# A decoder trunk step: shift, scale and h in two halves of the channels, with sample states on row groups and moved transposes

## What is computed

```
mod = silu(c) @ w_ada + b_ada
sh1, sc1, g1, sh2, sc2, g2 = split(mod, 6)
h = rmsnorm(x, norm_pre1) * (1 + sc1) + sh1
bg, cg, ua, q, k, v, r, lr, ga, gb = split(h @ w_in, ...)
y_a = bg * causal_dwconv(cg * ua)
log_a = log_sigmoid(lr @ w_a2 + b_a) / 16
S_t = diag(exp(log_a_t)) S_{t-1} + k_t^T v_t;  o_t = q_t S_t      # 4 heads, 128 x 256 states
y_b = rmsnorm(o) * silu(r)
x = x + g1 * rmsnorm((sigmoid(ga) * y_a + sigmoid(gb) * y_b) @ w_out, norm_post1)
h2 = rmsnorm(x, norm_pre2) * (1 + sc2) + sh2
a, gt = split(h2 @ w_up, 2)
x = x + g2 * rmsnorm((gelu(causal_dwconv(a)) * gt) @ w_down, norm_post2)
```

## Time and profile before

| | us |
|---|---|
| median of 3 runs | 1036.38 (1033.21 to 1036.59) |
| the profiled execution | 1031.13 |
| its span, first to last instruction | 1029.4 |
| PE busy | 1004.1 |
| DVE, ACT, POOL busy | 458.1, 368.2, 352.2 |
| mean granted clock of TensorE | 0.993 |

### The profile page before, as it was taken

One profiled execution on the slowest core, in us unless ns is written; L12 is line 12 of the kernel. 1 busy time (PEld: TensorE's weight loads), 2 busy tenths in 40 slices (PEclk: granted clock), 3 DMA queues, 4 the chain that ended last, 5 costly groups with the idle time before them and its releaser, 6 DMA issues.

```text
span 1029.4 us, 19196 instructions
## 1 busy us (share of the span) xinstructions
PE 1004.1 (98%) x7823; PEld 909.4 (88%) x7823; DVE 458.1 (45%) x664; ACT 368.2 (36%) x556; POOL 352.2 (34%) x174
## 2 busy tenths in 40 slices
PE   7799999999999999999999989999999999999997
PEld 5499889999999999989988779999999999888886
DVE  2410204575666554534556767545544445300204
ACT  4433532233434342544443434333333333212212
POOL 2033433242433333233342034333344333333330
PEclk9999999999999999999999989999999999999999
DMA  9658333756664566545354023322222222222212
GB/s 347 173 81 200 106 87 85 142 96 143 176 161 119 134 159 96 135 105 120 103 160 143 1 79 93 95 82 82 82 82 82 82 82 89 74 82 82 84 69 92
DMA packets 143858, 115.33 MB, mean 112 GB/s; under 512 B 11098, under 2 KB 123506, under 8 KB 142770
## 3 DMA queue, kind: packets, MB, share of 16 engines
q1 hardware_dynamic: 143697, 114.38, 42.1%
q10 hardware_dynamic: 96, 0.04, 0.0%
HBM read 107.02 MB, written 7.35 MB: 111 GB/s over the span
## 4 chain that ended last, share of the span: by engine, by line
PE 92%; SPq 3%; DVE 3%; ACT 1%; issue 1%; DMA 0%; DVEq 0%; ACTq 0%
PE pair L1546 60%; PE pair L1598 16%; PE pair L1873 4%; SPq L586 2%; PE pair L1678 1%; PE pair L1651 1%; PE pair L1533 1%; PE pair L1773 1%; SPq L624 1%; PE pair L1590 1%; PE pair L1741 1%; PE pair L1730 1%; PE pair L1591 1%; PE pair L1592 1%; PE pair L1589 1%; SPq L626 1%
## 5 line engine op out<-in xcount | busy, mean ns | idle before, releaser
L761 POOL TENSOR_TENSOR w_lo<-raw,w_hi 128x1024 fp32r<-128x1024 f32 x108 | 263.5, 2441 | 493.9 <-ACT w_hi L827 493.8
L1546 PE MATMUL pair<-h_hi,w_hi 128*128 128x288 f32 x1568 | 346.3, 299 | 1.8 <-DVE h_lo L568 1.8
L1546 PE MATMUL pair<-h_hi,w_lo 128*128 128x288 f32 x1568 | 340.0, 295 | 0.0
L1546 PE MATMUL pair<-h_lo,w_hi 128*128 128x288 f32 x1568 | 339.7, 295 | 0.0
L1546 PEld LDWEIGHTS pair<-h_hi,w_hi 128*128 128x128 f32 x1568 | 253.7, 189 | 19.6 <-issue 16.0
L1546 PEld LDWEIGHTS pair<-h_hi,w_lo 128*128 128x128 f32 x1568 | 254.1, 189 | 0.0
L1546 PEld LDWEIGHTS pair<-h_lo,w_hi 128*128 128x128 f32 x1568 | 254.0, 189 | 0.0
L827 ACT ACTIVATE w_hi<-raw 128x1024 fp32r<-128x1024 f32 x110 | 116.1, 1058 | 173.9 <-PE pair L1592 98.8
L761 POOL TENSOR_TENSOR w_lo<-raw_c,w_hi 128x1024 fp32r<-128x1024 f32 x24 | 66.8, 2786 | 130.9 <-ACT w_hi L827 130.9
L441 DVE SCALAR_TENSOR_TENSOR cv<-ext,ffp,cv 128x592 f32<-128x592 f32 x44 | 83.0, 1886 | 5.7 <-DVE cv L438 3.0
L1598 PE MATMUL pair<-w_hi,f_hi 128*128 128x512 f32 x176 | 68.8, 391 | 0.0
(11 more groups left out here) (305 smaller groups left out, 1144.0 us busy)
## 6 DMA issues: line engine op xcount, KB each, us to landing
raw<-in_w_up SPq DMA_DIRECT2D x44, 512.0 KB, 3.8
raw<-in_w_in SPq DMA_DIRECT2D x256, 64.0 KB, 3.2
raw_c<-in_w_ada SPq DMA_DIRECT2D x32, 512.0 KB, 5.4
raw_c<-in_w_in SPq DMA_DIRECT2D x192, 64.0 KB, 4.1
raw<-in_w_down SPq DMA_DIRECT2D x22, 512.0 KB, 3.4
ada_first<-in_w_ada SPq DMA_DIRECT2D x8, 1024.0 KB, 13.9
raw<-in_w_in SPq DMA_DIRECT2D x8, 512.0 KB, 5.3
s_in<-in_state_gla SPq DMA_DIRECT2D x8, 512.0 KB, 5.9
```

The lines of the kernel that those rows point to most:

```text
L761: pool.tensor_tensor(lo, raw_tile(n)[:, :], hi.bitcast(F32), ALU.subtract).then_inc(S("w_lo_done"), 1)
L1546: ins = pe.matmul(bank[pair][:, half, 0:HALF], w[:, i, :], x[:, i, HALF * half:HALF * half + HALF], start=i == 0 and p == 0, stop=i == KT ...
```

## The change

The shift and scale columns are loaded in two halves of the channels (0 to 511, then 512 to 1023), 16 transfers in place of 8, and rows, transposes, shift, scale, h32, h_hi and h_lo are made for one half, then for the other. In SP's queue key tile 0, the low-rank weights and key tiles 1 and 2 stand among the blocks of the second half. PE does its key passes over the first four channel blocks of three key tiles between the ada rows of the second half, then the last four blocks. Key tile 2 gets a raw buffer of its own, all low parts are POOL's, and the decay matmuls stand behind tiles 2 to 5. The parameter transposes go to another bank and the sample deltas of a head become one step: eight matmuls on groups of 32 rows into four banks, with states loaded and stored in two pieces each. DVE normalises ahead of the sample states. Between the projections the order of DVE, ACT and PE changes around the last two token tiles, and at the down projection four token tiles go ahead of the wait and the transposes. The core of the diff:

```diff
-    k_own = place("k_own", [P, NS // 2, DK], offset=g_at + 93184)
+    k_own = place("k_own", [P, 2, DK], offset=g_at + 93184)
...
-        if TILE_C1 <= n < TILE_WO and n % 4 > 1:
+        if n == 2 or TILE_C1 <= n < TILE_WO and n % 4 > 1:
...
+    def delta_at(u, s):
+
+        return one_bank((6, 7, 5, 4)[s])[:, DV * (u % 2):DV * (u % 2) + DV]
+
+    def sample_of(u, s):
+
+        return 4 * (s // 2) + 2 * (u % 2) + s % 2
...
-            if MIXED[x] == NCH:
+            x_stats(x)
+            if x > 0:
                 h2_high(x - 1)
-                x_stats(x)
-            else:
-                x_stats(x)
-                if x > 0:
-                    h2_high(x - 1)
...
+            def load_ada_first(i, half):
+
+                src = w_ada[P * i:P * i + P, 0:2 * D].rearrange("p (s h c) -> p s h c", s=2, h=2)
+                dst = ada_first[:, i, :].rearrange("p (s h c) -> p s h c", s=2, h=2)
+                sp.dma_start(dst[:, :, half, :], src[:, :, half, :]).then_inc(S(f"ada_in{4 * half + i // 2}"), 16)
+
             for i in range(KT):
-                sp.dma_start(ada_first[:, i, :], w_ada[P * i:P * i + P, 0:2 * D]).then_inc(S(f"ada_in{i}"), 16)
+                load_ada_first(i, 0)
                 for dst, src in small[3 * i:3 * i + 3]:
                     sp.dma_start(dst, src).then_inc(S("rows_in"), 16)
             load_raw(TILE_K, in_cols(IN_K))
             sp.dma_start(w_lr[:, :, 0:RANK], w_in[:, IN_LR:IN_LR + RANK].rearrange("(k p) c -> p k c", p=P)) \
               .then_inc(S("lr_in"), 16)
+            load_ada_first(0, 1)
             load_raw(TILE_K + 1, in_cols(IN_K + DK))
+            for i in (1, 2):
+                load_ada_first(i, 1)
+            load_raw(TILE_K + 2, in_cols(IN_K + 2 * DK))
+            for i in range(3, KT):
+                load_ada_first(i, 1)
             sp.wait_ge(S("lr_zero"), 2)
             for g in range(4):
                 sp.dma_start(w_a2[32 * g:32 * g + RANK, :], a["w_a2"][0]).then_inc(S("a2_in"), 16)
 
-            for h in range(2, HEADS):
-                load_raw(TILE_K + h, in_cols(IN_K + h * DK))
+            load_raw(TILE_K + 3, in_cols(IN_K + 3 * DK))
             for h in range(HEADS):
...
-            pool.wait_ge(S("w_lo_done"), 2)
-            for n in (2, 3):
+            for n in range(4):
...
+            def h_high(i):
+                if i % 4 == 0:
+                    act.wait_ge(S("h32_act"), i // 4 + 1)
+                    act.wait_ge(S("h_smp"), i // 2 + 2)
                 else:
-                    act.activation(h32[:, i, 0:SEQ], h32[:, i, 0:SEQ], ACT.Identity, bias=mod[:, i, 0:1],
-                                   scale=mul1[:, i, 0:1]).then_inc(S("h32_act"), 1)
-                    act.wait_ge(S("h32_act"), i - 3)
+                    act.wait_ge(S("h32_done"), 3 * (i // 4) + i % 4)
                 act.activation(h_hi[:, i, :], h32[:, i, :], ACT.Copy).then_inc(S("h_hi_done"), 1)
...
+            for half in range(2):
+                act.wait_ge(S("ada0_mm"), half + 1)
+                act.activation(rows_ada0[:, 0:256], one_bank(7)[:, 0:256], ACT.Copy).then_inc(S("rows0_done"), 1)
+                i = 4 * half
+                act.wait_ge(S("mul1_done"), 3 * (half + 1))
+                act.activation(h32[:, i, 0:SEQ], h32[:, i, 0:SEQ], ACT.Identity, bias=mod[:, i, 0:1],
+                               scale=mul1[:, i, 0:1]).then_inc(S("h32_act"), 1)
+                h_high(i)
+                if half == 0:
+                    high(0)
+                for x in range(1, 4):
+                    h_high(i + x)
+                if half == 0:
                     high(1)
-            high(2)
+                    high(2)
...
-                if n < 4:
-                    act.wait_ge(S("z_mm"), n + 1)
-                    act.activation(halves(suf[:, n, :]), out2(3), ACT.Abs, bias=prm[:, B_A + n:B_A + n + 1]) \
+                if 2 <= n < 6:
+                    z = n - 2
+                    act.wait_ge(S("z_mm"), z + 1)
+                    act.activation(halves(suf[:, z, :]), out2(3), ACT.Abs, bias=prm[:, B_A + z:B_A + z + 1]) \
...
-                sigmoid_r(1)
-                if not last:
-                    high(n + 6)
                 act.wait_ge(S("o_sq"), TT * h + TT)
                 act.activation(st_o[:, 1, 0:NCH], st_o[:, 0, 0:NCH], ACT.Sqrt, bias=eps[:, :], scale=1.0 / DV) \
                    .then_inc(S("o_root"), 1)
                 act.activation(st_o[0:64, 1, NCH:TT], st_o[0:64, 0, NCH:TT], ACT.Sqrt, bias=eps[0:64, :], scale=1.0 / DV) \
                    .then_inc(S("o_root"), 1)
+                sigmoid_r(1)
+                if not last:
+                    high(n + 6)
...
+            for half in range(2):
+                blocks = slice(4 * half, 4 * half + 4)
+                dve.wait_ge(S("back0"), half + 1)
+                for b in range(2):
+                    back = one_bank(7)[:, 256 + P * b:256 + P * b + P].rearrange("p (s g n) -> p s g n", s=2, g=2)[:, :, :, 0:9]
+                    dve.tensor_tensor(quarter(mod[:, 0:16, :], half, b), back, spread(quarter(prm[:, 0:16], half, b), 9),
+                                      ALU.add).then_inc(S("mul1_done"), 1)
+                dve.wait_ge(S("mul1_done"), 3 * half + 2)
+                dve.scalar_tensor_tensor(mul1[:, blocks, :], mod[:, 8 + 4 * half:12 + 4 * half, :], 1.0,
+                                         spread(prm[:, PRE1 + 4 * half:PRE1 + 4 * half + 4], 9), ALU.add, ALU.mult) \
+                   .then_inc(S("mul1_done"), 1)
+                dve.wait_ge(S("mul1_done"), 3 * half + 3)
+                if half == 0:
+                    dve.wait_ge(S("x_ch"), TT)
+                h_smp = h32[:, blocks, SEQ:T].rearrange("p k (s t) -> p k s t", t=TS)
+                dve.tensor_tensor(h_smp, h_smp, spread(mul1[:, blocks, 1:9], TS), ALU.mult).then_inc(S("h_smp"), 1)
+                dve.wait_ge(S("h_smp"), 2 * half + 1)
+                dve.tensor_tensor(h_smp, h_smp, spread(mod[:, blocks, 1:9], TS), ALU.add).then_inc(S("h_smp"), 1)
+                for i in range(4 * half + 1, 4 * half + 4):
+                    dve.tensor_scalar(h32[:, i, 0:SEQ], h32[:, i, 0:SEQ], mul1[:, i, 0:1], mod[:, i, 0:1], ALU.mult, ALU.add) \
+                       .then_inc(S("h32_done"), 1)
+                dve.wait_ge(S("h_smp"), 2 * half + 2)
+                for i in range(4 * half, 4 * half + 4):
+                    dve.wait_ge(S("h_hi_done"), i + 1)
+                    dve.wait_ge(S("h32_done"), 3 * (i // 4) + i % 4)
+                    dve.tensor_tensor(h_lo[:, i, :], h32[:, i, :], h_hi[:, i, :].bitcast(F32), ALU.subtract) \
...
-                sample_states(2 * h)
-                silu(1)
-                sample_states(2 * h + 1)
...
                     dve.tensor_scalar(o_tok[0:m, c, :], o_tok[0:m, c, :], st_o[0:m, 2, c:c + 1], None, ALU.mult) \
                        .then_inc(S("o_norm"), 1)
+                sample_states(2 * h)
+                silu(1)
+                sample_states(2 * h + 1)
...
+            for x in range(TT):
+                if x < TT - 2:
+                    if x > 0:
+                        h2_scale(dve, x - 1)
+                    y_part(dve, x)
+                else:
+                    if MIXED[x] == NCH:
+                        y_sum(dve, x)
+                    y_part(dve, x)
                     h2_scale(dve, x - 1)
                 if x > 0:
                     h2_shift(dve, x - 1)
+                xn_part(dve, x)
                 if x > 0:
                     h2_low(dve, x - 1)
+            h2_scale(dve, TT - 1)
+            h2_shift(dve, TT - 1)
+            h2_low(dve, TT - 1)
...
+            def ada_first_rows(i, half):
+                pe.wait_ge(S(f"ada_in{4 * half + i // 2}"), 32)
                 for g in range(4):
-                    ins = pe.matmul(one_bank(0)[32 * g:32 * g + 32, :], c_wide[:, i, :], ada_first[:, i, 512 * g:512 * g + 512],
+                    c0 = D * (g // 2) + 512 * half + 256 * (g % 2)
+                    ins = pe.matmul(one_bank(7)[32 * g:32 * g + 32, 0:256], c_wide[:, i, :], ada_first[:, i, c0:c0 + 256],
                                     start=i == 0, stop=i == KT - 1)
                 if i == KT - 1:
                     ins.then_inc(S("ada0_mm"), 1)
 
+            def ada_first_back(half):
+                pe.wait_ge(S("rows0_done"), half + 1)
+                for b in range(2):
+                    ins = pe.transpose(one_bank(7)[:, 256 + P * b:256 + P * b + P], rows_ada0[:, P * b:P * b + P], ident[:, :])
+                ins.then_inc(S("back0"), 1)
...
+            def key_pass(n, p):
+
+                pe.wait_ge(S("w_lo_done" if p == 1 else "w_hi_done"), n + 1)
+                for i in range(4):
+                    if n == 0 and p != 1:
+                        pe.wait_ge(S("h_lo_done" if p == 2 else "h_hi_done"), i + 1)
+                    key_block(n, p, i)
 
...
+            key_pass(0, 0)
+            pe.wait_ge(S("mul1_done"), 2)
```

(67 more changed lines are left out.)

272 lines of the change are left out of this document (93 added, 179 removed).

## The result

The changed kernel takes 1041.6 us (median of 20 runs, 1034.0 to 1045.4), the kernel before 1036.7 us (20 runs, 1029.2 to 1039.4). The ratio is 1.0047, with a 95% interval of 1.0029 to 1.0065: slower by 3.0 to 6.7 us. I had forecast 1033.4 us, in a range of 1026.5 to 1038.5. The profiled execution of the changed kernel took 1040.09 us.

A forecast was written before the change was run, and what follows sets the result against it. PE bounds the kernel, busy 1004.1 of 1029.4 us. Start +1.4, heads -5.5, output to up projection +2.7, down projection -1.6 sum to -3.0: 1028.1 profiled, plus 5.25 to the median, 1033.4 us; range 1026.5 to 1038.5.

The forecast's parts named there:

- the landing of the second half of the shift and scale weights: Start: old 33.15 us plus key tiles 7.5, low-rank weights 1.3, smaller pieces 1.1 gives 43.0 us; bounds 40.5 and 57.
- the two arrivals at 33.1 and 49.6 us: Start: first pair of second-half blocks there at 33.1 us; PE's first key matmul of the second half of channels at 49.6.
- Rival 4: Start: 512-byte key-tile pieces delay the second-half weights; landing at 57 us, 1045.7 us; decides from 50.8 on; chance 0.08, slower.
- The decay wait: Start: PE waits 4.2 us at the second decay matmul, clock 1.5 more, as ACT stands at tile 5's high part.
- the rest of the start: Start up to the values without the second decay matmul's wait and clock, 5.7 us; whole start forecast at +1.4 us.
- The new wait: Start, second decay matmul: its chain takes 15.1 us while PE has 10.9 us of work, so PE waits 4.2 us.
- Rival 1: Start: the second decay matmul does not wait; price -5.7 us, 1027.7 us; chance 0.17.
- Heads: Sample states on four row groups save 4.2 us, the last head's 1.28 us wait goes: -5.5 us in all.
- rival 3: Heads: the four row groups work only two by two; price +4.2 us, 1037.6 us, no change; chance 0.11.
- Output to up projection: New orders between these projections: PE waits 2.7 us, then 4.2 for the fourth up tile, clock behind each: +2.7 us.
- rival 2: Output to up projection: the fourth up tile does not wait; price -5.7 us, 1027.7 us; chance 0.12.
- Down projection: Four token tiles ahead of the wait for the last product cover PE's idle stretch: -1.6 us, bounds 0 and -1.6.

The follow-up runs named there:

- experiment 6: Kernel of experiment 5 with the low-rank weights loaded behind the last shift and scale block, their product steps later: 1025.88 us, ratio 0.9905 to the kernel before.
- experiment 9: Low-rank weights late and key passes filling PE's waits, as edits to experiment 5's kernel, plus key tile 2 loaded behind the blocks: 1029.29 us, ratio 0.992.
- experiment 2: Changed kernel with ACT's absolute value ahead of the high part of the tile three further on, for four decay products: 1035.55 us, ratio 0.998.
- experiment 5: Changed kernel with the edits of experiment 2 and experiment 3 together: 1031.86 us, ratio 0.9949 to the kernel before.
- experiment 3: Changed kernel with the DVE, ACT and PE orders of the kernel before between output and up projection: 1037.34 us, ratio 0.9999.
- experiment 4: Kernel before with only the heads and down projection parts of the change: 1030.01 us, ratio 0.9945.
- experiment 1: Kernel before and changed kernel profiled and timed again, no edit: 1037.82 us, ratio 1.0001, and 1041.16 us, ratio 1.0033.

## Why the prediction was wrong

**The step that failed is the landing of the second half of the shift and scale weights**, "33.15 + 7.5 + 1.3 + 1.1 = 43.0 us", and with it the two arrivals at 33.1 and 49.6 us. In the changed kernel the first pair lands at 36.2 us and the last block at 48.8, and the second half of the channels begins at 54.75. The first half of the weights was no part of the error: it was there at 23.3 us. (I had 24.1; the terms of the 43.0 give 23.4.)

Two things in the sum were too small. The low-rank weights, 1.3 us by estimate, put off the last landing by 4.0 us (experiment 6). And without them the forecast would be 41.7 us where the traces have 45.3: another 3.6 us are lost on the three key tiles at 2.5 us and the eight blocks at 1.35. I do not know on which. One key tile, taken out, was worth 1.3 us for the last pair, and put off the first pair by more than 3 (experiment 9), so a sum of costs one behind the other does not describe this queue. Rival 4 had the right place, and its key tiles may hold part of those 3.6 us; its mark, a landing from 50.8 us on, was not reached (48.8 and 50.5 in the two profiles).

PE also had less in hand than I thought. It waited at the first pairs already, and the granted clock, for which I had put 1.5 us, stayed at 0.50 from 30.6 to 40.9 us. That clock, with landings that differ by 1 to 2 us, is why the start varies so much from one execution to the next.

The start was thus worth more than the +6.3 of the two first profiles. Values begin at 107.24, 111.98 and 108.80 us in the three profiles with the changed start, and at 100.93, 102.58 and 102.75 in three with the old one: +7.3 us on average. The decay wait is 5.2 of that by experiment 2, and I had foreseen it. What I had foreseen wrongly is the rest of the start: it was to win 4.3 us (1.4 less 5.7) and wins nothing, with values at 102.09 and 101.45 us once the decay wait is gone (experiments 2 and 5).

**The new wait** of 4.2 us: 4.15 us, with the releaser, the cycle and the clock as worked out. Rival 1 (no wait) is out.

**Heads** -5.5: -5.7. The row groups work four at a time, so rival 3 is out. Stores and loads in two pieces made nobody wait.

**Output to up projection** +2.7: +3.0 by the profiles, and the old orders won 4.5 us by the profiles (3.0, and 1.5 for a clock that did not fall this time) and 5.0 us by the timed ratios (experiment 3). The waits came at 2.69 and 4.01 us, for the reasons given; rival 2 is out. DVE's addition at the start of POOL's low part took 3.30 us again, as in the row of 590.32 us, with both inputs in SBUF. The Trainium skill, SBUF — State Buffer, Who interferes with whom, has such an instruction contend with one of POOL that reads SBUF, and whoever issues first keeps the shared ports for its whole instruction; the trace agrees, with 3.30 us where 1.23 is normal.

**Down projection** -1.6: -1.6, and -1.7 in experiment 4.

**The sum.** +7.3 + 1.1 - 5.7 + 3.0 - 1.6 = +4.1 us, which lies in both timed intervals (3.0 to 6.7, and 0.6 to 6.3 in experiment 1). The 1.1 is the stretch between values and first sample outputs, 0.7, 1.4 and 1.3 us longer in the three profiles with the changed start, where I had put 0 without a reason. More than half of it is idle time: in every profile with the new start PE stands once or twice between 227 and 252 us, for 0.3 to 1.2 us in all, with nothing that it is seen to wait for, and in the three with the old start never. I did not find its cause.

The +9.0 of the two profiled spans holds 6.4 us of pitch that, by experiment 2, is not the change's: the profiled execution of before had the short pitch, that of the changed kernel the long one. My sum was made against the former and shifted to the median, which took care of it by luck.

**Open**: what decides about the pitch in an execution; why the last block lands 3.6 us late even without the low-rank weights, and SP stands for 6.4 to 7.6 us over the last five blocks at 240 to 290 GB/s when the first half went at 363; and by which way the 1024 small pieces take their time. Their own records give them 11 ns each, 0.7 us of all 16 engines, so it is not the time in which they are moved.
